# Sixteen groups of throwaway matmuls ahead of the first matmul of a two-block model

## The reference

```
h = x + gla_mixer(rmsnorm(x))            # q, k, v, r, g_low = rmsnorm(x) @ gla_w_in
x1 = h + relu(rmsnorm(h) @ mlp_w_up)^2 @ mlp_w_down
x1 = rmsnorm(x1)
proj = rmsnorm(x1) @ w_in_2              # q, k, v, xr, gr, three conv inputs, three gates
x2 = x1 + (g_a*attn + g_b*lru + g_c*conv) @ w_out_2
y  = rmsnorm(x2 + relu(rmsnorm(x2) @ w_mlp_up_2)^2 @ w_mlp_down_2)
```

## Time and profile before

| | us |
|---|---|
| median of 2 runs | 2767.69 (2766.48 to 2768.9) |
| the profiled execution, whole time | 2769.68 |
| its span, first to last instruction | 2767.6 |
| TensorE busy | 2735.8 |
| VectorE busy | 1796.9 |
| ScalarE busy | 1354.1 |
| POOL busy | 86.7 |

### The profile page before, as it was taken

The page is one execution under the profiler, slowest core; times in us unless marked ns, Lnnn a source line. Parts: engine busy times, 40 slices in busy tenths (PEclk is TensorE's granted clock), DMA queues, the critical chain, the costliest instruction groups (busy, mean ns, idle before and its releaser), DMA issues.

```text
span 2767.6 us, 43587 instructions
## 1 busy us (share of the span) xinstructions
PE 2735.8 (99%) x15627; PEld 2373.3 (86%) x15627; DVE 1796.9 (65%) x2073; ACT 1354.1 (49%) x1632; POOL 86.7 (3%) x69
## 2 busy tenths in 40 slices
PE   8999999999999999999999999999999999999998
PEld 7888888888888888888888888888888888888887
DVE  6666777656566567756777666666666565565664
ACT  4546555444444445444675554554454444444443
POOL 3000010000000002100000000000100000000001
PEclk9999999999999999999999999999999999999999
DMA  6564656656566565665455555555555565555653
GB/s 184 158 204 127 195 188 184 196 187 191 185 188 194 188 186 190 196 201 168 143 167 183 190 182 182 185 189 193 184 183 184 187 183 189 184 187 187 186 182 129
DMA packets 507074, 504.45 MB, mean 182 GB/s; under 512 B 17731, under 2 KB 505432, under 8 KB 506984
## 3 DMA queue, kind: packets, MB, share of 16 engines
q1 hardware_dynamic: 505820, 501.60, 56.9%
q10 hardware_dynamic: 1164, 1.63, 0.2%
HBM read 499.50 MB, written 3.67 MB: 182 GB/s over the span
## 4 chain that ended last, share of the span: by engine, by line
PE 94%; DVE 3%; ACT 1%; issue 1%; POOL 0%; DVEq 0%; POOLq 0%; ACTq 0%
PE acc L478 58%; PE acc L480 29%; PE acc L473 3%; PE acc L475 2%; DVE wsp L1008 1%; DVE lat L1287 0%; PE misc L578 0%; PE misc L593 0%; ACT wsp L751 0%; PE misc L535 0%; DVE z L1016 0%; PE misc L697 0%; PE misc L494 0%; POOL ssq L434 0%; PE misc L560 0%
## 5 line engine op out<-in xcount | busy, mean ns | idle before, releaser
L1008 DVE TENSOR_TENSOR wsp<-raw,wsp 128x1024 fp32r<-128x1024 f32 x944 | 1167.4, 1244 | 616.9 <-ACT wsp L751 588.1
L478 PE MATMUL acc<-xs,wsp 128*128 128x512 f32 x4224 | 1494.1, 399 | 8.0 <-DVE wsp L1008 7.9
L751 ACT ACTIVATE wsp<-raw 128x1024 fp32r<-128x1024 f32 x944 | 992.9, 1057 | 727.9 <-PE acc L480 670.4
L480 PE MATMUL acc<-xs,wsp 128*128 128x256 f32 x4224 | 1182.9, 280 | 0.0
L478 PEld LDWEIGHTS acc<-xs,wsp 128*128 128x128 f32 x4224 | 795.3, 188 | 203.4 <-DVE wsp L1008 9.6
L478 PE MATMUL acc<-hs,wsp 128*128 128x512 f32 x2560 | 897.9, 396 | 0.0
L480 PEld LDWEIGHTS acc<-xs,wsp 128*128 128x128 f32 x4224 | 798.6, 189 | 0.5
L480 PE MATMUL acc<-hs,wsp 128*128 128x256 f32 x2560 | 714.1, 279 | 0.0
L478 PEld LDWEIGHTS acc<-hs,wsp 128*128 128x128 f32 x2560 | 480.5, 188 | 115.4
L480 PEld LDWEIGHTS acc<-hs,wsp 128*128 128x128 f32 x2560 | 482.1, 188 | 0.0
L760 ACT ACTIVATE corr<-acc 128x512 f32<-128x512 f32 x248 | 148.3, 598 | 415.7 <-PE acc L480 396.3
(11 more groups left out here) (212 smaller groups left out, 1025.8 us busy)
## 6 DMA issues: line engine op xcount, KB each, us to landing
raw<-in_w_in SPq DMA_DIRECT2D x224, 512.0 KB, 4.1
raw<-in_mlp_w_up SPq DMA_DIRECT2D x128, 512.0 KB, 3.9
raw<-in_mlp_w_down SPq DMA_DIRECT2D x128, 512.0 KB, 3.3
raw<-in_w_mlp_up SPq DMA_DIRECT2D x128, 512.0 KB, 3.9
raw<-in_w_mlp_down SPq DMA_DIRECT2D x128, 512.0 KB, 3.3
raw<-in_gla_w_in SPq DMA_DIRECT2D x96, 512.0 KB, 3.7
raw<-in_gla_w_out SPq DMA_DIRECT2D x32, 512.0 KB, 4.3
raw<-in_w_out SPq DMA_DIRECT2D x32, 512.0 KB, 3.3
```

Source lines behind the costliest of these rows:

```text
L478: pe.matmul(acc[:, g, j], wsp[:, slot, t, 0, cols], x[:, k0 + k], start=start, stop=False, skip_group_check=True)
L480: ins = pe.matmul(acc[:, g, j, 1], wsp[:, slot, t, 1, cols], x[:, k0 + k, 0], start=False, stop=stop, skip_group_check=True)
L751: act.activation(wsp[:, slot, :, 0], raw[:, slot], ACT.Copy).then_inc(hi_done, 1)
L1008: dve.tensor_tensor(wsp[:, slot, :, 1], raw[:, slot], wsp[:, slot, :, 0].bitcast(F32), ALU.subtract).then_inc(lo_done, 1)
```

## The change

The tensor `warm` (128 partitions x 4096 f32) is laid over the second half of `arena_z`, and `warm_far` (128 x 128) over `arena_m`. POOL zeroes the lower half of `warm` ahead of all its other work and VectorE zeroes `warm_far` and the upper half ahead of its own. TensorE waits for both and then does 16 groups of eight matmuls into the second buffer of `acc`, alternating between its two banks, ahead of its first waits and its first transpose. Their results are overwritten later by the matmul with `start` set. The groups differ in the layout of the moving operand, the weights or the output.

```diff
+    warm = at("warm", [P, 4096], F32R, offset=arena_z + 16 * KB)
+    warm_far = at("warm_far", [P, P], F32R, offset=arena_m)
...
+    warm_lower, warm_upper = sem("warm_lower"), sem("warm_upper")
...
     @block.gpsimd
     def _(pool):
         own = Steps(pool, pool_steps)
+        pool.memset(warm[:, 0:2048].bitcast(F32), 0.0).then_inc(warm_lower, 1)
+        pool.wait_ge(warm_lower, 1)
         own.done(pool.memset(ident[:], 0.0))
...
+        pe.wait_ge(warm_lower, 1)
+        pe.wait_ge(warm_upper, 1)
+
+        def apart(lo, n, size, odd):
+
+            return warm[:, lo:lo + 2 * n].rearrange("p (g h s) -> p g h s", h=2, s=size)[:, :, odd]
+
+        def warm_up(weights, moving, n=512, m=P, backwards=False):
+
+            for i in range(8):
+                to = acc[0:m, 1, i % 2].rearrange("p a b -> p (a b)")[:, 0:n]
+                if backwards:
+                    to = to[:, ::-1]
+                pe.matmul(to, weights, moving, start=(i < 2), stop=(i > 5), skip_group_check=True)
+
+        plain, wide = warm[:, 0:P], warm[:, 1024:1536]
+        warm_up(plain, wide)
+        warm_up(plain, wide)
+        warm_up(plain, warm[:, 1024:1280], n=256)
+        warm_up(plain, wide[:, ::-1], backwards=True)
+        for size in (4, 8, 16, 32, 64, 128):
+            warm_up(plain, apart(1024, 512, size, 0))
+        warm_up(warm[:, 0:2 * P:2], wide)
+        warm_up(warm[:, 0:4 * P:4], wide)
+        warm_up(warm_far[:], wide)
+        warm_up(warm[:, 0:64], wide, m=64)
+        warm_up(plain, warm[:, 1024:2048:2])
+        warm_up(plain, warm[:, 1024:1028].unsqueeze(1).to_broadcast([P, P, 4]))
         pe.wait_ge(const_done, 2)
         pe.wait_ge(gain_landed, 16)
         pe.transpose(M[3][:, 0, 0:KT], stage[0:KT, 0], ident[0:KT, 0:KT]).then_inc(par_mm, 1)
...
+        dve.memset(warm_far[:].bitcast(F32), 0.0)
+        dve.memset(warm[:, 2048:4096].bitcast(F32), 0.0).then_inc(warm_upper, 1)
         dve.wait_ge(par_mm, 1)
         dve.tensor_copy(par[:, 0:KT], M[3][:, 0, 0:KT]).then_inc(par_done, 1)
```

## The result

The changed kernel takes 2800.58 us (2799.6 and 2801.56), the kernel before 2767.69: 32.9 us or 1.2% more by these medians. The ratio given with them is 1.0174, with an interval of [1.011, 1.0238], larger than the quotient of the two medians. The span of the profiled execution grew from 2767.6 to 2797.0 us, by 29.4. The forecast was 28.8 more, 2796.5 us within 2788 to 2815. So the medians lie in the range and the two spans nearly agree with the sum, while the ratio says 1.7% (by it the kernel before would become 2816 us, just above the range), and its interval leaves out the forecast's 1.0104. Both had to be explained: the 29.4 by the terms, and the ratio by what differs between executions of one and the same kernel.

What follows compares the result with a forecast made beforehand. TensorE, busy 99%, was taken as the bound, with VectorE's chain setting the head. Start 3.0, matmuls 29.3 and low clock 2.0 end the block at 34.3 us; with 0.8 and 24.7, unit 3 comes 28.8 later: 2796.5 us, range 2788 to 2815.

Steps and rivals of the forecast that it cites:

- the sum: Whole kernel: unit 3 begins at 59.8 instead of 31.0 us, so 28.8 us are added to the median 2767.7, giving 2796.5.
- The start: Head: TensorE's throwaway matmuls, waiting for two memsets, start between 2.6 and 3.4 us; 3.0 taken.
- the 4.5 taken: Beginning of the block: array at 1.2 GHz for 4.5 us, judged by transpose spacing, losing 2.0 us.
- The plain price: Throwaway block: 0.237 us per contiguous 512-column matmul at the high clock, taken for all layouts; 120 make 28.4 us.
- The head behind the block: From VectorE's first copy to unit 3: 24.7 us kept, after 0.8 us for first transpose and first pair.
- a weight load outlasts its matmul: Two groups with stepped weights: no cost below 237 ns; if loads took 376 ns, 2.2 us more.
- the cover: Head units: TensorE's waits for VectorE hide unit length and clock; without them at most 2.3 us per unit.
- the old distances: Everything behind the head: expected 29 us later, with spacing unchanged from the kernel before.
- The f32 price for nine groups: Rival, block: nine groups with stepped, blocked, repeated or reversed moving operand at f32 price, 17.5 us more, 2814; chance 0.11.
- a low clock under the whole block: Rival, block: clock stays low throughout, 52.9 us instead of 31.3, total 2818; chance 0.03.
- the two together: Rival, block: nine groups at half rate and TensorE held at 1.2 GHz, 52 us more, 2849; chance 0.05.
- the issue pieces: Rival, chain: instruction fetches move and "issue" (1% of span, 28 us) goes, total 2769; chance 0.04.

Runs made afterwards that it cites:

- e2: Changed kernel with memsets and TensorE's waits kept but all 128 throwaway matmuls left out; ratio 1.0009, nine executions around 2745.8 us, three around 2767.5.
- e1: The changed kernel run again unaltered, beside the kernel before; 2776.89 to 2780.2 us and 2798.24 to 2800.45 us, ratio 1.0153.
- e9: Kernel before plus a plain f32 matmul call pair ahead of mix stage, output projection and second MLP; median 2750.27 us, ratio 0.9989.
- e10: Changed kernel plus a plain f32 matmul call pair ahead of mix stage, output projection and second MLP; median 2780.24 us, ratio 1.0087.
- e3: Sixteen plain throwaway matmuls in TensorE's wait ahead of unit 0, none at the head; six executions around 2747.0 us, six around 2768.8, ratio 1.0018.
- e5: Changed kernel with four plain groups of eight instead of the sixteen groups; eight executions around 2754.8 us, two around 2778.6, ratio 1.0012.
- e4: Changed kernel with sixteen groups of eight in other layouts (steps, blocks, reversed, stepped weights, plain f32) at the head; one execution, 2790.97 us.
- e8: Kernel before plus one transpose ahead of each of nine loops of the second MLP; 2753.81 to 2756.64 and 2762.62 to 2767.49 us, ratio 1.0011.
- e11: Kernel before plus 12 throwaway matmuls in each of two later TensorE waits and three plain f32 call pairs; median 2746.59 us, ratio 0.9967.
- e6: Changed kernel with all sixteen groups reading the moving operand at step 2; 2800.94 us and three around 2826.0, ratio 1.0222.
- e7: Kernel before plus 12 throwaway matmuls in each of two later TensorE waits, none at the head; 2740.41 us and twelve around 2766.3, ratio 1.0028.

## Why the prediction was right, and where it failed

**The mechanism was right.** The block pushes the first transpose back, VectorE's chain behind it keeps its length, and nothing later takes up more than 1.7 us of the delay in the profiled pair. The end is 29.4 us later in the profiled pair, 30.2 in e2 and e1, and 30.0 in e9 and e10, where 28.8 was the sum. e2, e3 and e5 show separately that the memsets are free, that plain throwaway matmuls in a wait are free, and that a block of 9.4 us moves unit 3 by 7.0.

**The terms.** The start was 3.29 for 3.0: VectorE's memset of 2048 columns took 1.76 us, within the bounds of the earlier trace rows, but began only at 1.38. The clock was low until 7.26 us, by the distance of the starts, 4.0 us for the 4.5 taken; the transposes of the earlier trace rows were the right witness and the recorded 1.00 of the earlier trace rows was not. The plain price was 0.233 for 0.237. The head behind the block took 25.3 for 25.5. The prediction would have added the time by which a weight load outlasts its matmul; the loads of step 4 took 0.31 us, longer than the 0.237, and added nothing (1.88 us for the group, as for its neighbours). Two terms were put at nothing and weren't. The step-2 group cost 0.45 per matmul, 1.7 us more than plain; the forecast took the contiguous price for all layouts because "only the addresses differ", and its rival took the higher one for nine groups where it holds for one. And the clock's second fall came in unit 3, out of the cover, 1.5 us. The prediction named 2.3 us per unit as the price should the cover be gone, but said that it would stay; e2 and e3 show that even without the block it doesn't always. That the end comes within a microsecond or so of the sum is in part luck: unit 3 is 30.1 us later instead of 28.8, the eight f32 matmuls behind the head 31.1, and 1.7 comes back further on, by a low stretch and a rhythm of the stream that no term had.

The rule of the Trainium skill, in "PSUM — Partial Sum Buffer" (Specifications), that non-contiguous patterns in PSUM slow matmuls significantly, is not borne out, as far as a reversed or a stepped output falls under it: the reversed output took 0.23 per matmul in e4, and plain f32 into an output of step 2 took 0.216 per instruction of 256 columns (L543), the rate of the contiguous 0.43 per 512 (L557). What costs is the read side. The Trainium skill, in "SBUF — State Buffer" (the note on cachelines under "Door 1: The DMA port swizzle"), says that two hits on a 16-byte line suffice for full bandwidth; by it step 2 of a 4-byte type would be free, and here it took twice the time.

**The step that failed** is the last one of the sum, "the median 2767.7 becomes 2796.5". It takes the time of the kernel as one number and adds the shift of the head to it, with "the old distances" behind it. The runs showed two levels of one kernel instead: 2746.0 and 2769.0 us before, 2778.3 and 2799.1 after (e1). The prediction put the stream at 353 ns per pair, from a place where it ran so the earlier trace rows; elsewhere in the same trace it runs at 346.7, and which of the two the second half of an execution gets moves the total by 23 us, three quarters of the whole effect. Within a level the change costs 30.1 to 32.3 us (e1), but a ratio over a mixture of levels says something else. The executions shown of before, at 2766 to 2770, all lay in the upper level, and one trace of them couldn't say that there is another. That the rhythm makes the levels is shown (e1 against the profile after, e8, e9 to e11). That it also made the first ratio of 1.0174 is the likely reading, as in e1, where both levels of both kernels are seen and the same kind of ratio says 1.5% for what is 1.1%; the executions behind the first ratio aren't all shown, so this stays argued.

**The rivals.** The f32 price for nine groups, a low clock under the whole block and the two together did not happen (block of 32.5 us; e6). The loss of the issue pieces did not either. Issue has 2% of the chain instead of 1%, since the chain of the changed kernel puts the block itself down to it (start and length in us):

```profile
4.70 34.72 issue
```

## What to carry to other kernels

In these runs throwaway matmuls were free only inside a wait of TensorE, and even there the warm clock gained nothing where VectorE was the bound (e3), while in e7, where a low clock lay on the chain, fillers were worth some 2 to 5 us. Ahead of the first instruction of a chain that other engines then carry on, they cost their length less what the chain had waited anyway, however idle TensorE is later in that chain. Before a change of 1% is judged, look whether executions of the same kernel fall into levels, and compare level by level or make a variant that has only one. Count matmuls in equal windows of two traces of the same program: here that showed a difference of 2% in rate which no wait and no busy share shows.

## What the runs showed of the hardware

- A stream of fp32r matmuls of 512 and 256 columns runs at 346.7 or 353.3 ns a pair at the same granted clock. It kept this for over 1000 us, and changed where another kind of operation stood between (e8 at 2104 and 2557 us, e9 at 1527). With three plain f32 call pairs all 36 executions had the times of the faster one, and the three that have a trace show it; which of the pairs is needed and what decides are open.
- The place of a low stretch of the clock in the head differed between kernels that do the same work there: before at 26.2 us under unit 2, e2 at 31.9 in unit 3, where it cost 1.5 us.
- fp32r moving operands in runs of one or two elements with gaps between take 0.45 us per 512 columns at 1.2 and at 2.4 GHz alike (e4, e6); at 2.4 GHz runs of four and more, with gaps or without, and reversed ones take 0.23 to 0.24. Each element read twice takes 0.216, less than contiguous reading.
- Stepped weights load more slowly, 193 ns at step 2, 310 at step 4, 330 at step 8 and 300 at step 16 against 188, and this stays hidden or nearly so behind 512 columns: 0.235 us per matmul at step 4, 0.245 at step 8.
- A plain f32 call is two matmul instructions of 0.43 us per 512 columns each, 16 rows for eight calls at L557. The prediction's 0.48 per 512 from the earlier trace rows was the price of one instruction, not of a call.
